# Feed-forward products in seven multiplications instead of eight, over pairs of token blocks, in a two-layer decoder trunk

## The reference, cut to what matters

```python
def swiglu(h, w_gate_up, w_down):
    gu = h @ w_gate_up                      # (B, S, 2*D_FF)
    gate, up = gu[..., :D_FF], gu[..., D_FF:]
    return (jax.nn.silu(gate) * up) @ w_down
...
for i in range(DEPTH):
    x = x + 0.5 * swiglu(rmsnorm(x, norm_ffn[i, 0]), w_ffn_gate_up[i, 0], w_ffn_down[i, 0])
    h = rmsnorm(x, norm_mix[i])
    ...                                     # layer 0: pooling and convolution mixer; layer 1: short gated convolution
    x = x + mix
    x = x + 0.5 * swiglu(rmsnorm(x, norm_ffn[i, 1]), w_ffn_gate_up[i, 1], w_ffn_down[i, 1])
    gate = jax.nn.sigmoid(rmsnorm(x, norm_ple[i]) @ w_ple_gate[i])
    emb = rmsnorm(p[i].astype(x.dtype) @ w_ple_proj[i], norm_ple_proj[i])
    x = x + gate * emb
```

## Time and profile before

| | |
|---|---|
| three runs | 2616.43, 2616.8, 2830.22 us; median 2616.8 |
| the profiled execution | 2616.71 us, its span 2614.9 us (slowest of 8 cores, which lie between 2609.2 and 2614.9) |
| PE busy | 2567.1 us, 98% of the span, 14375 matmuls |
| DVE busy | 1154.5 us, 44% |
| ACT busy | 708.5 us, 27% |
| POOL busy | 168.4 us, 6%, of which most are weight transfers being issued |
| granted TensorE clock | 0.997 on average |

### The profile page before, as it was taken

One profiled execution on the slowest core, in us unless ns is written; L12 is line 12 of the kernel. 1 busy time (PEld: TensorE's weight loads), 2 busy tenths in 40 slices (PEclk: granted clock), 3 DMA queues, 4 the chain that ended last, 5 costly groups with the idle time before them and its releaser, 6 DMA issues.

```text
span 2614.9 us, 34970 instructions; the slowest of 8 cores (2609.2 to 2614.9 us)
## 1 busy us (share of the span) xinstructions
PE 2567.1 (98%) x14375; PEld 1245.1 (48%) x14375; DVE 1154.5 (44%) x2039; ACT 708.5 (27%) x1257; POOL 168.4 (6%) x254
## 2 busy tenths in 40 slices
PE   7999999999999999999999999999999999999996
PEld 2444544444454454444444454445444444544443
DVE  4432434756732222258722222267667322222687
ACT  5210112336621001125521001123334210011254
POOL 0000000012400000000000000000005000000000
PEclk9999999999999999999999999999999999999998
DMA  8220322055432132112042131102310321322113
...
DMA packets 53311, 127.18 MB, mean 49 GB/s; under 512 B 9504, under 2 KB 24608, under 8 KB 53024
## 3 DMA queue, kind: packets, MB, share of 16 engines
...
...
## 4 chain that ended last, share of the span: by engine, by line
PE 91%; DVE 5%; ACT 1%; DMA 1%; issue 1%; POOL 0%; SPq 0%; ACTq 0%; DVEq 0%; POOLq 0%
PE ps L558 91%; DVE x L528 1%; DVE g L528 1%; DMA ring<-wts 1%; DVE h L528 1%; DMA x<-xT 1%; DVE scr L528 1%; ACT L513 0%; DVE scr L521 0%; ACT scr L515 0%; DVE v L528 0%; ACT sq L515 0%; ACT h L515 0%; DVE x L521 0%; DVE hid L521 0%
## 5 line engine op out<-in xcount | busy, mean ns | idle before, releaser
L558 PE MATMUL ps<-g,ringh 128*128 128x512 f16 (+1 forms) x5280 | 973.2, 347 | 0.5 <-DVE scr L528 0.5
L558 PE MATMUL ps<-h,ring 128*128 128x512 bf16 (+1 forms) x4180 | 792.1, 349 | 26.2 <-DMA ring<-wts 13.8
L558 PEld LDWEIGHTS ps<-g,ringh 128*128 128x128 f16 x5280 | 472.3, 98 | 498.3 <-DVE scr L528 0.6
L515 ACT ACTIVATE scr<-ps 128x512 f32<-128x512 f32 (+1 forms) x610 | 319.1, 528 | 1246.1 <-PE ps L558 1217.6
L558 PEld LDWEIGHTS ps<-h,ring 128*128 128x128 bf16 x4180 | 375.3, 98 | 427.5 <-DMA ring<-wts 15.4
L521 DVE TENSOR_TENSOR hih<-ps,scr 128x512 f16<-128x512 f32 (+1 forms) x330 | 201.7, 611 | 730.7 <-PE ps L558 724.4
L558 PE MATMUL ps<-hih,ringh 128*128 128x512 f16 (+1 forms) x2640 | 489.4, 347 | 0.0
L558 PEld LDWEIGHTS ps<-hih,ringh 128*128 128x128 f16 x2640 | 236.8, 98 | 249.9
L528 DVE SCALAR_TENSOR_TENSOR x<-ps,x 128x512 f32<-128x512 f32 (+1 forms) x320 | 194.0, 609 | 330.8 <-PE ps L558 330.3
L515 ACT ACTIVATE sq<-x 128x512 bf16<-128x512 f32 (+1 forms) x313 | 171.0, 560 | 302.3 <-DVE x L528 255.5
L558 PE MATMUL ps<-hid,ring 128*128 128x512 bf16 (+1 forms) x1040 | 205.5, 348 | 0.6 <-DVE scr L528 0.5
...
## 6 DMA issues: line engine op xcount, KB each, us to landing
ringh<-wts POOLq DMA_DIRECT2D x72, 512.0 KB, 8.0
ring<-wts POOLq DMA_DIRECT2D x38, 512.0 KB, 7.8
ring<-wts POOLq DMA_DIRECT2D x22, 768.0 KB, 6.8
ringh<-wts POOLq DMA_DIRECT2D x18, 768.0 KB, 6.3
...
```

Source lines behind the costliest of these rows:

```text
L515: return e.activation(out=out, in_=in_, func=func, **kw)
L558: ins = e.matmul(o_, l, r, start=st, stop=sp)
```

## The change

Four things are changed together.

1. **Seven products for eight.** A gate/up product of one hidden tile over a pair of blocks (0 with 1, 2 with 3) and a down product of two output tiles over a pair are written as a 2x2 by 2x2 block product: the rows are the two blocks, the inner dimension is cut in halves, the columns are gate and up (or two output tiles). Each is formed from seven products of half the inner length (`gu_quad`, `dn_quad`), in Winograd's form, in which partial sums are shared. Weight combinations (`combine`, four tensor_tensor on POOL per weight tile) and input combinations (`try_T` for h, `hid_T` for the hidden tiles, on DVE, tiles ht and hit) are added. The bank A holds four results one after the other: it is read, and further matmuls add to it. In `gu_quad` the three read-outs are ACT copies to a scratch buffer; in `dn_quad` they are ACT copies which POOL adds to x (`via`), beside the four DVE updates (`upd`). The last product of a quad is emitted two products into the next one (`flush_group`). The sample block and the first four hidden tiles of the first FFN keep the plain product.
2. **Four parts.** D_FF is cut into 4, 6, 6 and 6 hidden tiles instead of 11 and 11, so x is updated four times per FFN. In the first three parts the down stage goes by output pair q, with both block pairs and the sample inside; in the last it takes pair (0, 1) for all four q, then pair (2, 3), then the sample.
3. **The ring** has 48 units of 256 columns and 48 more that are shared with ht, the embedding's buffers and others. A combined tile takes 7/4 of its loaded size. Three slots serve the gate/up tiles; the down tiles of the last part have fixed places 0, 11, 22, 33.
4. The first FFN is in float16 too, the early start of the next FFN (`advance`) is gone, and there are 8 scratch buffers for 5.

```diff
-HPARTS = [list(range(0, 11)), list(range(11, 22))]
-NHP = 11
+HPARTS = [list(range(0, 4)), list(range(4, 10)), list(range(10, 16)), list(range(16, 22))]
+NHP = 6
 TRI = ((0, 1, 2), (3, 4, 5), (6, 7))
-RUNIT = 1024
-NRUNIT = 18
+PAIRS = ((0, 1), (2, 3))
+RUNIT = 256
+NBASE = 48
+NEXT = 48
+NRUNIT = NBASE + NEXT
...
         def ffn(f):
             for hp, part in enumerate(HPARTS):
+                if f == 1 and hp == len(HPARTS) - 1:
+                    tiles.append((("plet", l), 8 * 256))
                 for m in part:
                     tiles.append((("gu", l, f, m), 8 * 256))
-                if f == 1 and hp == 1:
-                    tiles.append((("plet", l), 8 * 256))
-                for i in range(0, len(part), 3):
-                    ch = tuple(part[i:i + 3])
-                    tiles.append((("dn", l, f, ch), len(ch) * 1024))
+                for q in range(4):
+                    tiles.append((("dn", l, f, hp, q), len(part) * 256))
...
-            t = np.concatenate([_kc(w[:, m * 128:(m + 1) * 128]),
-                                _kc(w[:, DFF + m * 128:DFF + (m + 1) * 128])], axis=2)
+            g, u = w[:, m * 128:(m + 1) * 128], w[:, DFF + m * 128:DFF + (m + 1) * 128]
+            t = np.concatenate([_kc(g[:512]), _kc(g[512:]), _kc(u[512:]), _kc(u[:512])], axis=1)
         elif kind == "dn":
-            _, l, f, ch = key
+            _, l, f, hp, q = key
+            part = HPARTS[hp]
+            h = len(part) // 2
             w = inp["w_ffn_down"][l, f]
-            t = np.stack([w[c * 128:(c + 1) * 128, :] for c in ch], axis=1)
+            lo, hi = w[part[0] * 128:part[h] * 128], w[part[h] * 128:(part[-1] + 1) * 128]
+            c0, c1 = slice(q * 256, q * 256 + 128), slice(q * 256 + 128, q * 256 + 256)
+            t = np.concatenate([_kc(lo[:, c0]), _kc(hi[:, c0]), _kc(hi[:, c1]), _kc(lo[:, c1])], axis=1)
...
+    nc = bass.Bass("TRN2", target_bir_lowering=False, dynamic_dma_scratch_size=4096)
...
+    HT = [at(f"ht{p}", [128, 3, 4, 512], F16, "ring", ext0 + p * 12288) for p in range(2)]
...
-    SCR = Slots("scr", [alloc(f"scr{i}", [128, SCW], F32) for i in range(5)])
+    SCR = Slots("scr", [alloc(f"scr{i}", [128, SCW], F32) for i in range(8)])
...
+    def strassen(key):
+        return key[0] == "dn" or key[0] == "gu" and not (key[1:3] == (0, 0) and key[3] in HPARTS[0])
...
+        def _foot(self, k):
+            n = wt_off[k][1]
+            if strassen(k):
+                n = n * 7 // 4
+            return (n + RUNIT - 1) // RUNIT
...
+            if kind in ("oute", "outo", "pleg") and k[-1] != TRI[2]:
+                fixed = NBASE + 12 * TRI.index(k[-1])
+            elif kind in ("oute", "outo", "pleg"):
+                fixed = 0 if kind == "oute" else 40
+            elif kind == "dn" and k[3] == len(HPARTS) - 1:
+                fixed = 11 * k[4]
+            elif kind == "plep":
+                fixed = NBASE + EXT_US
+            elif kind in FIXED:
+                fixed = FIXED[kind][k[1] if len(k) > 1 else 0]
...
+            if kind == "gu" and strassen(k):
+                c = [i for i in (self.turn, self.turn + 14, self.turn + 28) if self.free(i % 42, 14)]
+                if c:
+                    self.turn = (c[0] + 14) % 42
+                return (c[0] % 42, 14) if c else None
...
-                rg = RING16 if k[0] in ("gu", "dn") and k[1:3] != (0, 0) else RING
-                dma("pool", rg[:, pl[0] * RUNIT:pl[0] * RUNIT + n], d_w[:, off:off + n], f"wsem{pl[0]}",
+                st = strassen(k)
+                rg = RING16 if k[0] in ("gu", "dn") else RING
+                base = pl[0] * RUNIT
+                dma("pool", rg[:, base:base + n], d_w[:, off:off + n], f"wsem{pl[0]}",
                     extra=self.extra.get(self.pos, ()))
-                self.loaded[k] = (pl, rg[:, pl[0] * RUNIT:pl[0] * RUNIT + n])
+                self.loaded[k] = (pl, rg[:, base:base + (n * 7 // 4 if st else n)])
                 self.pos += 1
+                self.land = max(pe_t[0] + 2.0, self.land) + 5.5 * n / 2048
+                if st:
+                    defer(self.land - pe_t[0], lambda k=k: self.combine(k), ("S", k))
+
+        def combine(self, k):
+            t = self.loaded[k][1]
+            q = wt_off[k][1] // 4
+            a = [t[:, i * q:(i + 1) * q] for i in range(7)]
+            pool_tt(a[4], a[0], a[3], ALU.subtract)
+            pool_tt(a[3], a[3], a[2], ALU.add)
+            pool_tt(a[5], a[3], a[0], ALU.subtract)
+            pool_tt(a[6], a[1], a[5], ALU.subtract)
...
+    def try_T(p):
+        if p in thold or not all(b in hready for b in PAIRS[p]) or not W.free(NBASE + 24 * p, 24):
+            return
+        W.ext = 0
+        b0, b1 = PAIRS[p]
+        hready.difference_update(PAIRS[p])
+        lo0, hi0, lo1, hi1 = H16[b0][:, 0:4, :], H16[b0][:, 4:8, :], H16[b1][:, 0:4, :], H16[b1][:, 4:8, :]
+        t1, t2, t4 = (HT[p][:, i, :, :] for i in range(3))
+        ops = [(t1, lo1, lo0), (t2, hi1, t1), (lo1, hi1, lo1), (t4, hi0, t2)]
+        for i, (o_, a, b) in enumerate(ops):
+            defer(1.2 * i, lambda o_=o_, a=a, b=b: dve_tt(o_, a, b, ALU.subtract), ("T", p))
+
+    def h_done(b):
+        if b == SB:
+            dve_tt(HTS[:, :, :], H16[b][:, 4:8, :], H16[b][:, 0:4, :], ALU.subtract)
+            return
...
+    def gu_quad(a, p, j, h):
+        b0, b1 = PAIRS[p]
+        r4 = range(4)
+        A = bank()
+        mm(A[:, :], [(a[0][k], H16[b0][:, k, :]) for k in r4], chain=True)
+        s1 = scr()
+        act(s1[:, 0:512], A[:, :], AF.Copy)
+        Dk = bank()
+        mm(Dk[:, :], [(a[3][k], HT[p][:, 0, k, :]) for k in r4], chain=True)
+        s3 = scr()
+        act(s3[:, 0:512], Dk[:, :], AF.Copy)
+        flush_group()
+        mm(A[:, :], [(a[5][k], HT[p][:, 1, k, :]) for k in r4], start=False, chain=True)
+        s2 = scr()
+        act(s2[:, 0:512], A[:, :], AF.Copy)
+        Bk = bank()
+        mm(Bk[:, :], [(a[1][k], H16[b0][:, 4 + k, :]) for k in r4])
+        dve_tt(s1[:, 0:512], Bk[:, :], s1[:, 0:512], ALU.add)
+        bfree(Bk)
+        act(s1[:, 0:512], s1[:, 0:512], AF.Silu)
+        mm(Dk[:, :], [(a[6][k], H16[b1][:, 4 + k, :]) for k in r4], start=False, chain=True)
+        dve_tt(s2[:, 0:512], Dk[:, :], s2[:, 0:512], ALU.add)
+        bfree(Dk)
+        act(s2[:, 0:512], s2[:, 0:512], AF.Silu)
+        mm(A[:, :], [(a[4][k], H16[b1][:, k, :]) for k in r4], start=False, chain=True)
+        dve_tt(s3[:, 0:512], A[:, :], s3[:, 0:512], ALU.add)
+        dve_tt(HID16[b1][:, j, :], s3[:, 0:512], s2[:, 0:512], ALU.mult)
+        sfree(s2)
+        sfree(s3)
+
+        def fin():
+            mm(A[:, :], [(a[2][k], HT[p][:, 2, k, :]) for k in r4], start=False, chain=True)
+            dve_tt(HID16[b0][:, j, :], A[:, :], s1[:, 0:512], ALU.mult)
+            bfree(A)
+            sfree(s1)
+            hid_T(p, j, h)
+        last_group[0] = fin
...
+    def hid_T(p, j, h):
+        b0, b1 = PAIRS[p]
+        if j < h:
+            dve_tt(HIDT[p][:, 0, j, :], HID16[b1][:, j, :], HID16[b0][:, j, :], ALU.subtract)
+            return
+        i = j - h
+        dve_tt(HIDT[p][:, 1, i, :], HID16[b1][:, j, :], HIDT[p][:, 0, i, :], ALU.subtract)
+        dve_tt(HID16[b1][:, i, :], HID16[b1][:, j, :], HID16[b1][:, i, :], ALU.subtract)
+        dve_tt(HIDT[p][:, 2, i, :], HID16[b0][:, j, :], HIDT[p][:, 1, i, :], ALU.subtract)
...
+    def dn_quad(a, p, q, h, nm):
+        b0, b1 = PAIRS[p]
+        m1, m2 = 2 * q, 2 * q + 1
+        r = range(h)
+        x0, x1 = X[b0], X[b1]
+
+        def via(bk, x):
+            t = scr()
+            act(t[:, 0:512], bk[:, :], AF.Copy, scale=0.5)
+            pool_tt(x, x, t[:, 0:512], ALU.add)
+            sfree(t)
+
+        def upd(bk, x, b, mo):
+            dve_stt(x, bk[:, :], 0.5, x, ALU.mult, ALU.add)
+            if nm is not None:
+                nm[b].chunk(mo)
+        A = bank()
+        mm(A[:, :], [(a[0][k], HID16[b0][:, k, :]) for k in r], chain=True)
+        via(A, x0[:, m1, :])
+        Dk = bank()
+        mm(Dk[:, :], [(a[3][k], HIDT[p][:, 0, k, :]) for k in r], chain=True)
+        via(Dk, x1[:, m2, :])
+        flush_group()
+        mm(A[:, :], [(a[5][k], HIDT[p][:, 1, k, :]) for k in r], start=False, chain=True)
+        via(A, x1[:, m1, :])
+        Bk = bank()
+        mm(Bk[:, :], [(a[1][k], HID16[b0][:, h + k, :]) for k in r])
+        upd(Bk, x0[:, m1, :], b0, m1)
+        bfree(Bk)
+        mm(Dk[:, :], [(a[6][k], HID16[b1][:, h + k, :]) for k in r], start=False, chain=True)
+        upd(Dk, x1[:, m1, :], b1, m1)
+        bfree(Dk)
+        mm(A[:, :], [(a[4][k], HID16[b1][:, k, :]) for k in r], start=False, chain=True)
+        upd(A, x1[:, m2, :], b1, m2)
+
+        def fin():
+            mm(A[:, :], [(a[2][k], HIDT[p][:, 2, k, :]) for k in r], start=False, chain=True)
+            upd(A, x0[:, m2, :], b0, m2)
+            bfree(A)
+        last_group[0] = fin
...
+            if fin:
+                assert W.ext == 0
```

(27 more changed lines are left out.)

388 lines of the change are left out of this document (234 added, 154 removed).

## The result

The changed kernel takes 2961.4 us (median of 4 runs, 2958.0 to 3195.4) against 2616.8 us before: a ratio of 1.131, 95% interval 1.129 to 1.134. The direction was forecast, the size was not: 107 us slower were expected, 345 came, far outside the range. For the change it is 2951 us against 2611 to 2612.

The account below looks back on a forecast made before the run. TensorE at full pace (98% busy) was taken as the bound: 2616.7 - 221 for fewer matmuls + 328 of new waits (90 + 72 + 56 + 78 + 20 + 12) = 2724 us, 4% slower; 8-in-10 range 2555 to 2790.

Parts of the forecast that it names:

- The gain: TensorE: 1024 fewer matmuls of 512 columns at 0.216 us each take 221 us off.
- The last stages: Each FFN's last down stage: first half held by POOL's combinations, 56 us; second half by DVE's work, 78 us in four.
- Who waits for whom: Down stages: TensorE waits for DVE's updates, DVE for POOL's additions; in last stages' first halves TensorE waits for POOL's combinations.
- The price of a combination: POOL: a 16-bit combination of weights costs 1.17 us per 512 columns, as in float32.
- rival 1: POOL's combinations are cheap, at half price: about 75 us less, 2648 us; chance 0.18.
- Rival 2: Down stages: queues average out, TensorE waits only for totals; 2516 to 2592 us; chance 0.15 (under 2564), 0.06 (to 2600).
- Rival 3: TensorE's clock falls at pauses: 20 us more in last stages' first halves, 28 in short stages; 2770 us; chance 0.13.
- The rounds of the down stages: Down stages: last products wait for the ACT, POOL, DVE chain; 90 us in four short (four-tile) stages, 72 in eight middle.
- The starts: First gate/up stages of later FFNs: first weights issued late, three starts of 4, 12 us; DVE's 2048-column steps hide.
- Free: fewer units: Fewer ring units, float16 in the first FFN and 3 more scratch buffers: nothing waits, no cost.
- Gate/up: Gate/up stages: the third DVE sum comes late while POOL combines; 20 us, between nothing and 55.
- at 38 to 44 us: Sign that the forecast is right: the time of each down stage of a short (four-tile) part.

Follow-up runs that it names:

- experiment 5: Changed kernel with sixteen 128-column matmuls ahead of the last product of every quad in short and middle down stages; die median 2967 us.
- experiment 2: Changed kernel without the four combinations of weights per tile, products reading the fetched quarters instead; die median 2817 us (kernel before 2629 there).
- Experiment 7: Changed kernel with plain products in gate/up and down, keeping its four parts, ring and order; die median 2711 us, ratio 1.036 to the kernel before.
- experiment 12: Changed kernel with DVE making a down quad's third addition, no weights combined, no blocks differenced; die median 2642 us (kernel before 2625 there).

## Why the prediction was wrong

**Right.** The direction. The gain: a plain six-tile gate/up stage takes 88.2 us and one in seven products 78.3, where nothing keeps TensorE waiting; 9.9 us for 48 matmuls, against 10.4 by my 0.216. The last stages: 134 forecast, 150 measured. Who waits for whom. The price of a combination came within 0.05 us, and with it rival 1 (half of that) is excluded. Rival 2, slack in the chain, shows in no stage. Rival 3's mechanism came: the granted clock was 0.81 to 0.97 in every down stage but one (1.00). Its price of 28 us for the short stages was too high, for raising the clock gave 5.6 there (experiment 5); its 20 us for the last stages are untested.

**The rounds of the down stages** (41 and 55 us short). "One round is: product A5 and last product ..." counts one of POOL's additions, and a second by the sentence behind it (5.0 and 4.4 us). That holds for a pair's second quad: 4.96 us in a middle stage of experiment 2 and 4.5 in a short one, where I had 5.0 and 4.4. It fails for the first. There the quad before has been finished, nothing overlaps, and three additions stand in a row behind the first copy of A. Worked again with the prediction's own durations: copy and three additions are 4.5 us, two DVE updates 1.3, two products and a result 1.1; that is 6.9 instead of the 5.7 (4.4 + 1.3) that I had. In the pair of experiment 2 shown above it was 6.97 us from last product to last product, and 5.37 for the other quad, at half the clock; in a middle stage it was 7.48 where I had 6.5. Without combinations a pair takes 12.0 (short) and 12.4 us (middle); I had 10.1 and 11.5: 61 us over all stages. The combinations took 10.5 us of each short stage and 5.2 of each middle one, not 8 and 2: 35 us. "Lie mostly where POOL idles" was the error. The sets cost 0.4 to 1.8 us behind a pair's last addition and 2.9 to 4.2 between its two quads, and I had counted two sets, eight combinations, per middle stage, where 11 combinations stand in the one at 1011.2 and 14 in the one at 1672.5.

**The starts** (57 short). The prediction says that the eight DVE steps of 2048 columns "hide behind the second pair's norm". The steps took the cheaper price that I had left open (1.22 us for 2048 columns, half of the 2.4), but they did not hide: without them the starts lose 23 us. Beside POOL they took about twice as long. VectorE in order of time at the second FFN's start, first in the change, then without combinations:

```profile
796.32 1.23 DVE L534 TENSOR_TENSOR scr<-scr,sq 128x128 f32<-128x128 f32 x1
797.47 2.72 DVE L534 TENSOR_TENSOR ht<-hh,hh 128x2048 f16<-128x2048 f16 x1
...
803.86 2.17 DVE L534 TENSOR_TENSOR ht<-hh,ht 128x2048 f16<-128x2048 f16 x1
805.95 1.23 DVE L534 TENSOR_TENSOR scr<-scr,sq 128x128 f32<-128x128 f32 x1
```

```profile
754.52 1.17 DVE L534 TENSOR_TENSOR scr<-scr,sq 128x128 f32<-128x128 f32 x1
755.62 1.21 DVE L534 TENSOR_TENSOR ht<-hh,hh 128x2048 f16<-128x2048 f16 x1
...
757.94 1.22 DVE L534 TENSOR_TENSOR ht<-hh,ht 128x2048 f16<-128x2048 f16 x1
759.08 0.29 DVE L534 TENSOR_TENSOR scr<-scr,sq 128x128 f32<-128x128 f32 x1
```

A 128-column sum of squares costs 0.29 us alone and 1.03 to 1.23 beside a POOL instruction (the first row of each list lies beside a POOL sum of squares, 805.95 beside combinations). I had priced the contention in the last stages and in gate/up, and not at the starts. It is the smaller part of them: without combinations the starts lose only 6 us, without differences 23, without both 35. What holds the other 24 is open. The Trainium skill (SBUF — State Buffer, "Who interferes with whom") has it as an exclusive lock for the length of the instruction that came first; the trace agrees, since the 0.29 us operation grows to about the length of POOL's (1.15 to 1.22 us), not in proportion.

**Left out** (48). "Free: fewer units ..., TensorE's order decides there and nothing waits" was wrong for the embedding: its sample block is fetched only after the block before it has been read, POOL stands in order before that transfer, and TensorE waits 9.4 us for it, twice. Experiment 7 shows it without any seven-product form.

**Gate/up** (24 short): the size of a term, put at 20 between 0 and 55; 44. Experiment 2 puts 33 of them to the combinations; 11 stay without, around two late fetches.

One sentence was wrong in itself: short stages "at 38 to 44 us" did not follow from my own 26 + 22 = 48.

**Not settled:** what still holds the short stages at 36.5 us in experiment 12, the starts 24 us and the last stages 106 us over full pace; and how far the low clock lengthens the starts and the last stages (0.87 and 0.84 in the windows above), which experiment 5 did not touch.
